# Second merge of a two-layer diffusion trunk: one group of three or four expert slots per step, five more selection parts beside attention, four weight blocks requested together

## The reference

```python
def trunk_layer(x, mod, lp, rope, ctx_kv):            # two layers; 128 context + 512 latent tokens
    h = rmsnorm(x, lp["norm1_g"]) * (1 + sc1) + sh1
    mix, ctx_tensors = mixer_block(h, lp, rope, ctx_kv)   # Fourier, convolution, attention, window attention
    x = x + g1 * mix
    h = rmsnorm(x, lp["norm2_g"]) * (1 + sc2) + sh2
    x = x + g2 * peer_ffn(h, ...)

# end of mixer_block: the "merge" and the output projection
merged = gates[:, :, 0] * y_f + gates[:, :, 1] * y_c + gates[:, :, 2] * y_a + gates[:, :, 3] * y_w
return merged @ lp["w_out"], ctx_tensors

# peer_ffn, for each 128 tokens: 8 heads, the best 16 of 16384 experts for each
s_half, i_half = lax.top_k(sc, 16)                    # the "selection"
top_s, top_pos = lax.top_k(cand, 16)
eidx = jnp.take_along_axis(cand_idx, top_pos, axis=-1)
gate = jax.nn.softmax(top_s, axis=-1)
u, v = u_tab[eidx], v_tab[eidx]                       # rows of 1024 numbers each
act = jax.nn.gelu(jnp.einsum("chkd,cd->chk", u, hc))
return jnp.einsum("chk,chkd->cd", (gate * act), v)
```

## Time and profile before

| | us |
|---|---|
| median of 3 runs | 5485.01 |
| the profiled execution, its own time | 5502.59 |
| its span, first to last instruction | 5500.8 |
| PE busy | 4392.1 (80%) |
| DVE busy | 3596.6 (65%) |
| ACT busy | 1252.1 (23%) |
| POOL busy | 1542.8 (28%) |
| row DMAs (queue 0), share of 16 engines | 61.7% |
| weight and other DMAs (queue 1) | 12.3% |

### The profile page before, as it was taken

One profiled execution on the slowest core, in us unless ns is written; L12 is line 12 of the kernel. 1 busy time (PEld: TensorE's weight loads), 2 busy tenths in 40 slices (PEclk: granted clock), 3 DMA queues, 4 the chain that ended last, 5 costly groups with the idle time before them and its releaser, 6 DMA issues.

```text
span 5500.8 us, 45164 instructions
## 1 busy us (share of the span) xinstructions
PE 4392.1 (80%) x13844; PEld 2483.3 (45%) x13844; DVE 3596.6 (65%) x7876; ACT 1252.1 (23%) x3024; POOL 1542.8 (28%) x1290
## 2 busy tenths in 40 slices
PE   7989999978878676666689899898898776666665
PEld 5846764444444222222267478544445442222222
DVE  1932177766667988876638312886676589888765
ACT  1132147611111111111111311565111111111111
POOL 0000013223331454455400000232233324454453
PEclk9989999989989888888889799999899898888887
DMA  4133458779986999999921334687899869999997
GB/s 166 61 129 134 142 206 313 281 284 348 354 340 227 368 419 421 422 421 422 379 98 54 121 115 139 244 313 268 298 360 354 325 230 393 421 421 421 421 422 302
DMA packets 227570, 1589.36 MB, mean 289 GB/s; under 512 B 26112, under 2 KB 28416, under 8 KB 47872
## 3 DMA queue, kind: packets, MB, share of 16 engines
q0 software_dynamic: 184320, 1342.26, 61.7%
q1 hardware_dynamic: 43008, 244.21, 12.3%
HBM read 1581.66 MB, written 4.72 MB: 288 GB/s over the span
## 4 chain that ended last, share of the span: by engine, by line
PE 40%; DMA 27%; DVE 21%; ACT 4%; issue 4%; DVEq 2%; POOL 1%; SPq 0%; POOLq 0%; ACTq 0%
DMA B<-tables,R 19%; PE ps L529 9%; PE ps L539 7%; DVE B L1561 6%; PE ps L681 5%; DMA A<-tables,R 4%; PE ps L586 4%; DVE A L1595 4%; PE ps L546 3%; PE ps L667 3%; DMA H<-tables,R 2%; PE ps L559 2%; DVE A L1561 2%; DMA B<-ws 1%; DVE H L1561 1%
## 5 line engine op out<-in xcount | busy, mean ns | idle before, releaser
L529 PE MATMUL ps<-B,R 128*128 128x512 f32 x2264 | 1267.0, 707 | 516.8 <-ACT R L970 515.8
L495 POOL DMA_INDIRECT B<-tables,R x788 | 933.0, 1184 | 2124.4 <-PE ps L529 978.8
L1561 DVE SCALAR_TENSOR_TENSOR B<-B,M 128x1024 f32<-128x1024 f32 x788 | 947.8, 1223 | 287.8 <-DMA B<-tables,R 269.8
L529 PEld LDWEIGHTS ps<-B,R 128*128 128x128 f32 x2264 | 485.5, 225 | 1201.7 <-ACT R L970 628.9
L539 PE MATMUL ps<-H,B 128*128 128x384 f32 (+1 forms) x2048 | 593.8, 444 | 21.6 <-DMA B<-ws 20.7
L529 PE MATMUL ps<-A,R 128*128 128x512 f32 x736 | 414.5, 705 | 187.5 <-ACT R L970 187.5
L495 POOL DMA_INDIRECT A<-tables,R x282 | 339.4, 1203 | 635.3 <-PE ps L529 440.0
L539 PEld LDWEIGHTS ps<-H,B 128*128 128x128 f32 x2048 | 400.6, 196 | 221.1 <-issue 56.7
L964 ACT ACTIVATE T<-T 128x2 f32<-128x2 f32 (+1 forms) x452 | 93.3, 206 | 1620.3 <-DVEq L1563 1618.9
L970 ACT ACTIVATE R<-cs,A 128x128 f32<-128x128 f32 x898 | 309.6, 395 | 588.7 <-DVEq L1584 588.7
L529 PE MATMUL ps<-H,R 128*128 128x512 f32 x544 | 315.8, 723 | 142.1 <-ACT R L970 142.1
(11 more groups left out here) (237 smaller groups left out, 5050.5 us busy)
## 6 DMA issues: line engine op xcount, KB each, us to landing
B<-ws SPq DMA_DIRECT2D x120, 1024.0 KB, 5.2
B<-ws SPq DMA_DIRECT2D x128, 768.0 KB, 4.4
B<-tables,R POOLq DMA_INDIRECT x788, 13.2
A<-tables,R POOLq DMA_INDIRECT x282, 13.6
R<-tabs SPq DMA_DIRECT2D x2, 2176.0 KB, 14.5
H<-tables,R POOLq DMA_INDIRECT x194, 11.2
x<-xin SPq DMA_DIRECT2D x1, 2560.0 KB, 9.2
y<-M SPq DMA_DIRECT2D x1, 2560.0 KB, 7.9
```

Source lines behind the costliest of these rows:

```text
L495: pool.indirect_dma_start(out=ring[s], out_offset=None, in_=tables[:, :], in_offset=bass.IndirectOffsetOnAxis(ap=EI[:, n:n + 1], axis=0),) ...
L529: mm = pe.matmul(ps[:, bk + c, :], diag[PE_AT[n] % DIAGS], v_row[:, c * 512:(c + 1) * 512], start=(n in PE_FIRST), stop=(PE_AT[n] + 1 == P ...
L1561: v.scalar_tensor_tensor(out=u_row, in0=u_row, scalar=1.0, in1=h2[:, g.tile, :], op0=ALU.mult, op1=ALU.mult, accum_out=dots[:, o:o + 1])
```

## The change

```diff
-MG_GROUPS = [(AT_MERGE + 3 * (s // 2) + s % 2, AT_MERGE + 3 * ((s + 1) // 2) + (s + 1) % 2) for s in range(N_MG)]
+MG_PLAN = [(3, 1), (3, 1), (4, 1)] + [(3, 1)] * 4 + [(4, 1)] + ([(3, 1)] * 11 + [(4, 2)]) * 2
+MG_GROUPS = [(AT_MERGE + s, AT_MERGE + s + 1) for s in range(N_MG)]
@@ def groups():
-    plan = [(2, 2)] * AT_MERGE + [(2, 1), (2, 1), (2, 0)] * (N_MG // 2) + [(2, 1)] * (AT_END - AT_OUT)
+    plan = [(2, 2)] * AT_MERGE + MG_PLAN + [(2, 1)] * (AT_END - AT_OUT)
@@
-SELECT_AT = [q for q in range(AT_OUT) if q >= AT_MERGE or q % 3 != 2][:len(SELECTS)]
+SELECT_AT = [q for q in range(AT_OUT) if q >= AT_MERGE or q % 4 != 3][:len(SELECTS)]
@@ def load(n):
-                    sp.wait_ge(w_used.sem, used(l, n) if n in range(BLOCKS, BLOCKS + WS) else
+                    sp.wait_ge(w_used.sem, used(l, BLOCKS) if n in range(BLOCKS, BLOCKS + WS) else
@@ def weighed(q):
                     if g.place in OPENS[g.tile]:
                         gates(g)
+                    weights(q)
                     if q in SELECT:
                         select(*SELECT[q])
-                    weights(q)
```

## The result

The changed kernel takes 5668.6 us (median of 4 runs, 5650.2 to 5672.2) where the kernel before, run beside it, takes 5489.0 (4 runs, 5474.6 to 5494.8). The ratio is 1.0327, 95% interval 1.031 to 1.0343: slower by 3.3%, some 180 us. The forecast was 5568, range 5455 to 5645. The sign was right and the size was not.

The account below looks back on a forecast made before the run. Late rows on the six-home ring were taken to bound the merge. Merge 34 + 37, attention 3, norm 9, tail 0 made +83 on 5502.6: 5586, or 5568 on the medians' scale; range 5455 to 5645.

Parts of the forecast that it names:

- The rival in which the ring doesn't bind: Merge: a pair of rows lands within about 6.5 us, TensorE sets the pace; 5371, or 5454 half late; chance 0.13.
- the cycle of 12.3 us: Merge: each step from the third on lasts 12.3 us, set by late rows, more than TensorE's 9.46; thirty steps, 369 us.
- the forecast's 413: Length of each merge in us: 21 + 369 + 18 + 5, against 379.2 and 376.3 before.
- the 1.4 us between requests: Merge: POOL needs about 1.4 us from one row request to the next, a link of the cycle.
- The rival with a cycle of 13.8: Merge: TensorE cools and the weight block falls between the two rows; 45 us more a layer, 5658; chance 0.08.
- Groups of four: Merge: the extra home is freed later by TensorE, its row comes at least 2.6 us after the third; seven times, 18 us.
- the residual: Merge: tile 0's residual, 5.1 us, stands between products and sums inside the chain, no longer hidden by TensorE's slack: 5 us.
- The norm: Second norm: slot 232 becomes first of its first group, weights 8 us later; counted 4.5 us a layer, bounds 0 and 8.
- Attention: Tiles 2 to 4: 7.5 - 7 - 2 + 3 = +1.5 us a layer, bounds -8 to +10.
- The tail: Tail: four slots fewer in its plan save nothing, since 372 rows are moved from slot 268 on, before and after.
- The loads: Merge: weight blocks requested together save 18 us a layer by themselves, but late rows already use this up.
- The scale: Whole kernel: the profiled execution's 5586 is carried to the median of runs, 17.6 lower, so 5568.

Follow-up runs that it names:

- e5_early_sums: The changed kernel, with VectorE adding up a merge group's rows right behind that group's own weights, not behind the next group's products: 5443.2 us, ratio 0.991.
- e12_threes_end: The changed kernel with 96 slots in the merge instead of 100, and early sums from the merge through the end of the keys: 5382.2 us, ratio 0.9809.

## Why the prediction was right and wrong

**What binds.** Right. The forecast said that a row added up by VectorE holds its home past the next group's products, and that two groups on six homes can't bear that. The chain of waits shows that loop, and e5_early_sums, which alters when the home is released, takes 225 us off, about what the grouping cost. With groups of two the same edit takes off 31 (5442.0 to 5410.8): it is the late release together with only two groups on the ring that costs so much. The rival in which the ring doesn't bind is out. By the formula of the Trainium skill, DMA: Bandwidth & Descriptors, Anatomy of one DMA, a lone row lands after 4.4 us and two after 6.8, an estimate from its figures; here the pair took 10.3 to 10.6 from the first request.

**The step that failed: the cycle of 12.3 us.** It measured 13.28 and 13.53. Over 30 steps that is 29 and 37 us a layer, of the 29 and 40 us by which the merges (442.4 and 452.7) exceed the forecast's 413. The largest piece is the 1.4 us between requests, taken from the pair of the earlier trace rows: it is 2.14 when the first of two sums releases the request, since that request then takes up to 1.86 us and not about 1. The landing took 8.2 to 8.4 where I had 8.0; the weight blocks are 0.3 of it. The release, 1.7, was right. So the wait that the forecast left out is that of POOL's request for the sum beside it. In the pair of the earlier trace rows, from which the 1.4 was read, the first request (1149.64) began when a sum had only 0.27 us left, and took 1.08:

```profile
1148.62 1.29 DVE L1595 SCALAR_TENSOR_TENSOR A<-A 128x1024 f32<-128x1024 f32 x1
```

The rival with a cycle of 13.8 was near in length and in its 5658, but for the wrong cause: it laid it on the weight block.

**Groups of four, and the residual.** Both terms were right. In the steps with three late homes the turn was 16.0 to 16.1, 2.5 to 2.8 over the others, for 2.6 forecast; the step with the residual of a tile lasted 17.9 and 18.2, so 4.6 over the others, for 5. With the measured turn the forecast's own sum reads 21 + 30 x 13.28 + 18 + 5 = 442, and 450 with 13.53. That it meets the measured 442 to the microsecond is partly luck: the products of the first two steps are done after 14 us where this sum has 21, and the turns of steps 2 to 5 are together 5 to 7 us longer than it has them.

**The norm.** The gross 8 us was about right (8.65). I then let short waits behind it take up half and wrote 4.5. Nothing took it up: with rows in time the four slots cost 11 us. That the late sums of the merge carry over into this stretch was in no term.

**Attention** was right in sum, +1.4 and -0.2 for +1.5, and its parts roughly so: the moved selection with weights ahead gave 3.2 and 1.5 where the terms say 1.5 (7.5 - 7 - 2), and the three weight blocks cost 6.2 and 5.2 where I had 3. **The tail** was right: four slots fewer in its plan shorten nothing. **The loads** were nearly right: worth 16 us in a merge of twos, and 8.0 and 5.3 in one of threes, where the sum had them used up. What I did not see is that the parts of the selection in the merge, ahead of the weights, cost 16 to 20 us a layer before; I only said that they would cost if the rows were early.

**The scale.** The forecast was carried from the profiled execution to the medians by taking off 17.6 us. That did not hold for the changed kernel, whose profiled execution lay at its median: in spans the miss is 84 us (167 for 83), of which 69 are the merges and 18 the norm, and in medians 100.

## What to carry to other kernels

Before a group is made larger, count how many groups the ring then holds, and how long each row is held after its last use: with two groups, any work between use and release is added to the full latency of the next request. Release a buffer behind its own use, not behind the next group's, even if the engine then waits for another; here the same grouping went from 5668.6 to 5443.2 us by that. When a chain is priced from a trace, take each link beside the same company that it will have, since a request beside a busy VectorE is not one beside an idle VectorE.

## What the runs showed of the hardware

POOL's indirect request of one row takes 0.93 to 0.95 us with VectorE idle (24 requests in the first merge of the changed kernel, 32 in its first tail). When it begins during a VectorE product or sum of 128 x 1024, which read two tensors in SBUF, it ends 0.81 or 0.82 us behind that instruction's end, in all 425 such cases there, and so takes up to 2.00 us. The Trainium skill, SBUF — State Buffer, Who interferes with whom, says that a VectorE instruction with two SBUF inputs contends with a GpSimd instruction that reads SBUF, that the port pair they share is an exclusive lock, and that the order of issue decides who blocks. In the kernel the request takes its row numbers from `EI`, a part of a tensor in SBUF. The traces agree: the request, which came second, waited for the whole rest of the instruction.

A row of 1 MB requested second of a pair needs 8.2 to 8.4 us to land, one of 0.5 MB 6.1 to 6.3; the line through the two leaves about 4 us for a row of no size, an estimate for this traffic. TensorE's granted clock was 0.90 and 0.88 in the merges of the changed kernel, where the engine was idle 95 us of each, and 0.99 in the first merge of e12_threes_end, where it was idle 12.
